# Two layers of a hybrid attention and convolution trunk: three taps of the depthwise convolution take later places on VectorE

## The chip, the cores and the metric

The kernel runs on one core of one Trainium2 chip. The metric is device time in microseconds (us) for one execution. TensorE does the matrix products, VectorE (DVE) and ScalarE (ACT) the elementwise work, GpSimd (POOL) small pieces, and SyncE (SP) issues the weight transfers.

## The reference, cut to what matters

Two layers, 512 rows of 1024 channels, float32. The change is about the order of the work of the depthwise convolution, a sum of 31 taps over each of 512 channels, and about the up-projection of latent attention, beside which some taps are computed.

```python
for l in range(DEPTH):                       # DEPTH = 2
    h = rmsnorm(x, norm_mix_g[l])
    proj = h @ w_in[l]                       # c_q, c_kv, k_r, q_b, k_b, v_b, f_logit, conv_in, gate_logit
    q_a = rmsnorm(c_q, q_norm_g[l]) @ w_uq[l]        # 384 -> 8 heads * (64 + 32 rotary)
    kv  = rmsnorm(c_kv, kv_norm_g[l]) @ w_ukv[l]     # 256 -> 8 heads * (64 keys + 64 values)
    o_a = block_attention(qa, ka, va, mla_scale, chunk_mask) @ w_bo_a[l]
    o_b = block_attention(qf, kf, vf, fox_scale, frame_mask, cum) @ w_bo_b[l]
    u = conv_in[..., :512] * sigmoid(conv_in[..., 512:])
    u = causal_depthwise_conv(u, dw_kernel[l], dw_bias[l])      # 31 taps a channel
    u = silu(layernorm(u, conv_ln_g[l], conv_ln_b[l]))
    o_c = u @ w_bo_c[l]
    y = g_a * o_a + g_b * o_b + g_c * o_c            # sigmoid gates from proj
    x = x + y @ w_out[l]
    h = rmsnorm(x, norm_ffn_g[l])
    x = x + (silu(h @ w_ffn_gate[l]) * (h @ w_ffn_up[l])) @ w_ffn_down[l]
return rmsnorm(x, final_norm_g)
```

## The kernel before

**Tiling.** Activations lie transposed: 128 channels on the partitions, 512 rows along the free dimension. A weight matrix is streamed in chunks of up to 128x1024 numbers. Each float32 number is split into a high part in a rounded matmul format and a low part, the rest, and each product is three matmuls: high by high, high by low, low by high.

**The path of a chunk.** SP loads it into one of four `raw` buffers. ScalarE casts it into one of two `w_hi` buffers (L686), once TensorE has finished the chunk that lies two before it. VectorE subtracts (L1069) and writes `w_lo`. TensorE waits for that (`lo_done`) and multiplies (L1557; in the value chunks L1609; in attention L1669). Results land in PSUM banks, and VectorE or ScalarE empties them.

**The order.** Every engine has its own list, written out by hand: there is no scheduler. A layer runs latent projections (8 chunks), convolution inputs (8), the up stage (8), attention with 18 chunks of projections mixed in, a first merge pass (28 chunks after the first 6), a second merge pass, the output projection and the feed-forward network.

**The up stage.** Its chunks are `UP` + 0 to 7. Chunks 0 and 1 give the rotary part of the queries, 2 and 3 its other part, 4 and 5 the keys (VectorE copies one tile of each, L1392, ScalarE the other, L915), 6 and 7 the values: together four tiles. In its turn c VectorE empties what it has to, then splits chunk c + 2, then computes `UP_TAPS[c]` taps. So turn 4 splits `UP` + 6, turn 5 splits `UP` + 7, turn 6 splits the first chunk of attention, and turn 7 splits nothing. Beside this GpSimd adds the rotary halves (L640), eight instructions in a row.

**The taps.** One tap is one VectorE instruction, `c_acc = u_pad[k:] * weight_k + c_acc` over 128x512 (L1146; the first tap of a channel group is L1143). There are 4 channel groups of 31 taps. Two taps in a row of one group wait for each other; of different groups they don't. All taps of the convolution stage and the up stage belong to group 0. Then `TAP_LIST` goes around the groups. The rest of the taps fill attention (`STEP_TAPS`, one to three between the softmax instructions) and 14 chunks of the first merge pass (`PASS1_TAPS`). After the last one VectorE adds the four groups (L1421) for the layer norm.

**The start of attention.** TensorE computes the scores of a step (L1624), VectorE the negated maximum (L1187), ScalarE the exponential (L780), VectorE the reciprocal and the scaling (L1157, L1159), TensorE the transposition (L1681). Three banks hold scores, so the scores of step 5 wait for the exponential of step 2. In between TensorE multiplies the projection chunks. VectorE's list has here: the maxima of steps 0 and 1, the split of the second chunk, a tap, the scaling of step 0, a tap, the scaling of step 1, a tap, and the maxima of steps 2 and 3.

The lines that pick the taps of the up stage and of the merge pass:

```python
                    if 2 <= c <= 6:
                        split(UP + c + 2)
                    for _ in range(UP_TAPS[c]):
                        tap(*next(taps_left))
...
                    split(MERGE + 2 * GATES_AHEAD + m + 2)
                    if turn is None:
                        for _ in range(PASS1_TAPS[m]):
                            tap(*next(taps_left))
```

Of the kernel before, what the change touches and what calls it, by code (L numbers as in the profile page):

```python
# [86 lines left out]


CONV_TAPS = (0, 0, 1, 1, 2, 2, 1, 0)
UP_TAPS = (0, 0, 1, 1, 0, 3, 1, 1)  # L90
LN_TURNS = 3
PASS2_TURNS = D // P // 2
CENTRE = ((), (0, 1), (2, 3), ())
# [8 lines left out]
GATES_AHEAD = 3  # L102
V_TURN_STEPS = {12: 0, 20: 1, 28: 2, 36: 3}
PASS1 = [(3, c) for c in range(4)] + [(j, c) for j in range(GATES_AHEAD) for c in (2, 3)] + [(j, c) for j in range(4, 8) for c in range(4)]
PASS1_TAPS = [3, 3, 2, 2] + [1] * 5 + [2, 5, 3, 1, 0]
STEP_TAPS = [1 + (g % 3 == 1) for g in range(62)] + [1, 1]
TAP_LIST = [(0, k) for k in range(sum(CONV_TAPS) + sum(UP_TAPS))]
TAP_LIST += [(c, k) for k in range(TAPS) for c in (1, 2, 3, 0) if (c, k) not in TAP_LIST]
STEP_TAPS[61] += CT * TAPS - sum(CONV_TAPS) - sum(UP_TAPS) - sum(PASS1_TAPS) - sum(STEP_TAPS)
assert min(STEP_TAPS) >= 0 and sum(FEED_UNITS) == 8 * len(FEED) + 6 and FEED_END[-1] == 61  # L110
# [107 lines left out]
def trunk(nc, dram, out):  # L218
# [121 lines left out]
    with ExitStack() as ctx:  # L340
# [703 lines left out]
        def _(dve):  # L1044
# [17 lines left out]
            def split(i):  # L1062

                size, kind = CHUNK_LIST[i % CHUNKS][:2]
                dve.wait_ge(hi_done, hi.add())
                h, last = w_hi[i % SPLIT], None
                for (to, of), (part, _) in zip(split_views(kind, size, w_lo[i % SPLIT], raw[i % RAW]),
                                               split_views(kind, size, h, raw[i % RAW])):
                    last = nc.vector.tensor_tensor(to, of, part.bitcast(F32), ALU.subtract)  # L1069
                last.then_inc(lo_done, 1)  # L1070
# [65 lines left out]
            def tap(c, k):  # L1136


                if taps.n % (CT * TAPS):
                    dve.wait_ge(tap_done, taps.value - (last_tile[0] not in (None, c)))  # L1140
                last_tile[0] = c
                if k == 0:
                    ins = nc.vector.tensor_scalar(c_acc[:, c, :], u_pad[:, c, 0:T], dwk_l[:, c, 0:1],  # L1143
                                                  par[:, R_DWB + c:R_DWB + c + 1], ALU.mult, ALU.add)
                else:
                    ins = nc.vector.scalar_tensor_tensor(c_acc[:, c, :], u_pad[:, c, k:k + T], dwk_l[:, c, k:k + 1],  # L1146
                                                         c_acc[:, c, :], ALU.mult, ALU.add)
                ins.then_inc(tap_done, 1)
                taps.add()
# [138 lines left out]
            for l in layers([(hi, CHUNKS - 2), (mm, EVENTS), (out_n, EVACS), (own, OWN), (taps, CT * TAPS), (sg, 4 + 24 + 22),  # L1288
# [80 lines left out]
                for c in range(UP_CH):  # L1369
# [24 lines left out]
# [4 lines that stand above are left out]
# [3 lines left out]
                for m, (j, c) in enumerate(PASS1):  # L1401
# [12 lines left out]
# [3 lines that stand above are left out]
                    if m == len(PASS1_TAPS) - 1:  # L1417
                        dve.wait_ge(tap_done, taps.value)
# [550 lines left out]
```

## Time and profile before

| | |
|---|---|
| time, median of 3 | 1721.35 us (1721.31 to 1721.38) |
| span of the profiled execution | 1719.7 us |
| TensorE busy | 1707.8 us, 99% |
| VectorE busy | 1080.4 us, 63% |
| ScalarE busy | 684.5 us, 40% |
| GpSimd busy | 195.9 us, 11% |
| share of TensorE in the chain that ended last | 94% |
| up stage to the start of attention | about 92 to 121 us in layer 0, 939 to 968 us in layer 1 |

The profile is of one execution, whose span is 1.65 us below the median of the timed runs. In a timeline, a row gives start, length, engine, line, operation and, in brackets, how long the engine stood idle before it and who ended that. Records of neighbours on one engine overlap by up to about 0.1 us, and TensorE's by more, since matmuls are pipelined: there the distance of two starts counts.

### The profile page before, as it was taken

What the parts mean: (1) busy time and instruction counts of PE and PEld (TensorE: products, weight loads), DVE (VectorE), ACT (ScalarE), POOL (GpSimd) and SP (SyncE); (2) the same over time, 40 slices, a digit from 0 to 9 for tenths busy, and PEclk for the clock granted to TensorE, in tenths of its full rate; (3) what the DMA queues carried; (4) which work ended last, traced back from release to release, by engine and by line L of the source; (5) the groups of instructions that cost most, each with busy time, mean ns of one, the idle gap of its engine ahead of it and who ended that gap; (6) DMA issues with size and microseconds to landing.
All of it is one profiled execution on the core that took longest, in us unless ns stands there. A gap on an engine that the chain in (4) does not pass through costs nothing.

```text
span 1719.7 us, 22100 instructions
## 1 busy us (share of the span) xinstructions
PE 1707.8 (99%) x7908; PEld 1367.4 (80%) x7908; DVE 1080.4 (63%) x1625; ACT 684.5 (40%) x1126; POOL 195.9 (11%) x124
## 2 busy tenths in 40 slices
PE   9999999999999999999999999999999999999998
PEld 7777777878888888888878777778788888888887
DVE  6898887966555555542359998877755555555223
ACT  4655544343343332322245554453434423333222
POOL 0831000010020000001126210000001100000010
PEclk9999999999999999999999999999999999999999
DMA  6341221433433333333243322113333333333331
GB/s 166 82 106 52 60 62 31 111 86 98 113 89 98 98 98 98 95 92 101 81 102 71 92 62 60 45 55 100 92 104 109 98 94 93 95 96 95 93 98 71
DMA packets 309909, 152.18 MB, mean 88 GB/s; under 512 B 30356, under 2 KB 309134, under 8 KB 309836
## 3 DMA queue, kind: packets, MB, share of 16 engines
q1 hardware_dynamic: 309528, 150.96, 31.7%
q8 instruction: 45, 0.74, 0.2%
q10 hardware_dynamic: 308, 0.25, 0.1%
q14 instruction: 28, 0.23, 0.0%
HBM read 149.09 MB, written 2.10 MB: 88 GB/s over the span
## 4 chain that ended last, share of the span: by engine, by line
PE 94%; DVE 3%; ACT 1%; POOL 1%; DMA 1%; issue 0%; SPq 0%; ACTq 0%; POOLq 0%; DVEq 0%
PE bank L1557 71%; PE bank L1669 12%; PE bank L1702 2%; PE bank L1681 2%; PE bank L1624 2%; PE bank L1640 1%; PE bank L1904 1%; DVE w_lo L1069 1%; PE bank L1609 1%; POOL ln_acc L566 1%; DMA raw<-in_w_in 1%; PE bank L1596 1%; PE bank L1587 0%; PE bank L1645 0%; ACT w_hi L686 0%
## 5 line engine op out<-in xcount | busy, mean ns | idle before, releaser
L686 ACT CAST w_hi<-raw 128x1024 fp32r<-128x1024 f32 (+3 forms) x311 | 295.1, 949 | 711.4 <-PE bank L1557 704.5
L1069 DVE TENSOR_TENSOR w_lo<-raw,w_hi 128x1024 fp32r<-128x1024 f32 (+3 forms) x311 | 347.2, 1116 | 205.1 <-ACT w_hi L686 203.9
L1557 PE MATMUL bank<-h_hi,w_hi 128*128 128x512 f32 x1184 | 466.3, 394 | 0.7 <-DVE w_lo L1069 0.4
L1557 PE MATMUL bank<-h_hi,w_lo 128*128 128x512 f32 x1184 | 461.1, 389 | 0.0
L1557 PE MATMUL bank<-h_lo,w_hi 128*128 128x512 f32 x1184 | 460.9, 389 | 0.0
L1557 PEld LDWEIGHTS bank<-h_hi,w_hi 128*128 128x128 f32 x1184 | 222.2, 188 | 55.4 <-issue 6.2
L1107 DVE TENSOR_TENSOR tmp<-bank,rstd_x 128x512 f32<-128x512 f32 x140 | 96.7, 690 | 260.4 <-PE bank L1557 252.8
L1557 PEld LDWEIGHTS bank<-h_lo,w_hi 128*128 128x128 f32 x1184 | 222.4, 188 | 46.9 <-issue 1.9
L1557 PEld LDWEIGHTS bank<-h_hi,w_lo 128*128 128x128 f32 x1184 | 222.3, 188 | 46.3
L1146 DVE SCALAR_TENSOR_TENSOR c_acc<-u_pad,dwk_l,c_acc 128x512 f32<-128x512 f32 x240 | 188.3, 802 | 0.4
L566 POOL TENSOR_TENSOR x_acc<-x_acc,x_sq 128x512 f32<-128x512 f32 x31 | 53.3, 1721 | 866.0 <-ACT x_sq L703 534.0
L1669 PE MATMUL bank<-h_hi,w_hi 128*128 128x512 f32 x304 | 130.9, 431 | 0.0
L1557 PE MATMUL bank<-f_hi,w_hi 128*128 128x512 f32 x330 | 128.9, 391 | 0.0
L1557 PE MATMUL bank<-f_hi,w_lo 128*128 128x512 f32 x330 | 128.5, 389 | 0.0
L1557 PE MATMUL bank<-f_lo,w_hi 128*128 128x512 f32 x330 | 128.4, 389 | 0.0
L1669 PE MATMUL bank<-h_hi,w_lo 128*128 128x512 f32 x304 | 119.0, 391 | 0.0
L1669 PE MATMUL bank<-h_lo,w_hi 128*128 128x512 f32 x304 | 118.6, 390 | 0.0
L780 ACT ACTIVATE p_b<-bank,neg_max 128x384 f32<-128x384 f32 (+3 forms) x128 | 66.8, 525 | 73.9 <-DVE neg_max L1187 72.2
L753 ACT COPY p_t<-bank 128x384 f32<-128x384 f32 (+3 forms) x128 | 49.4, 428 | 97.3 <-PE bank L1681 58.0
L1187 DVE TENSOR_REDUCE neg_max<-bank 128x1 f32<-128x384 f32 (+3 forms) x128 | 58.1, 485 | 37.7 <-PE bank L1645 24.2
L1557 PEld LDWEIGHTS bank<-f_hi,w_lo 128*128 128x128 f32 x330 | 62.0, 188 | 13.0
L1557 PEld LDWEIGHTS bank<-f_hi,w_hi 128*128 128x128 f32 x330 | 62.0, 188 | 12.7
(263 smaller groups left out, 2218.4 us busy)
## 6 DMA issues: line engine op xcount, KB each, us to landing
raw<-in_w_in SPq DMA_DIRECT2D x96, 512.0 KB, 3.8
raw<-in_w_ffn_gate SPq DMA_DIRECT2D x44, 512.0 KB, 3.7
raw<-in_w_ffn_up SPq DMA_DIRECT2D x44, 512.0 KB, 3.7
raw<-in_w_ffn_down SPq DMA_DIRECT2D x32, 512.0 KB, 3.8
raw<-in_w_out SPq DMA_DIRECT2D x16, 512.0 KB, 3.8
raw<-in_w_ffn_down SPq DMA_DIRECT2D x16, 384.0 KB, 3.4
raw<-in_w_bo_a SPq DMA_DIRECT2D x16, 256.0 KB, 2.7
raw<-in_w_bo_b SPq DMA_DIRECT2D x16, 256.0 KB, 2.7
```

Of the source, the lines that this page charges most:

```text
L566: nc.gpsimd.tensor_tensor(acc[:], acc[:], ring[i % 2][:], ALU.add).then_inc(sq_added, 1)
L686: last = nc.scalar.copy(to, of)
L753: nc.scalar.copy(to, t_bank[g % 2][:, 0:(q + 1) * P].rearrange("p (k q) -> p k q", q=P)).then_inc(turn_out, 1)
L780: nc.scalar.activation(p_b[:, p_at:p_at + w], s_bank[score_slot(step)][:, 0:w], ACT.Exp, bias=neg_max[:, step % 4:step % 4 + 1], accum_out ...
L1069: last = nc.vector.tensor_tensor(to, of, part.bitcast(F32), ALU.subtract)
L1107: return nc.vector.tensor_tensor(to, s_bank[b][rows, :], by[rows, :], ALU.mult)
L1146: ins = nc.vector.scalar_tensor_tensor(c_acc[:, c, :], u_pad[:, c, k:k + T], dwk_l[:, c, k:k + 1], c_acc[:, c, :], ALU.mult, ALU.add)
L1187: nc.vector.tensor_reduce(neg_max[:, n:n + 1], s_bank[score_slot(step)][:, 0:(q + 1) * P], AX_X, ALU.max, negate=True).then_inc(max_ready, 1)
L1557: ins = nc.tensor.matmul(bank_t[0:rows, :], wt[slot][:, w], x, start=first and k == 0 and p == 0, stop=last and k == k_tiles - 1 and p == 2)
L1624: nc.tensor.matmul(s_bank[score_slot(g)][:, 0:w], q_t[0:rows, head, q * P:w], k_t[0:rows, head, 0:w], start=True, stop=True).then_inc(scor ...
L1669: ins = nc.tensor.matmul(bank_t[:], wt[(QKV + n) % SPLIT][:, w], x, start=k == 0 and p == 0, stop=k == DT - 1 and p == 2, skip_group_check ...
L1681: ins = nc.tensor.transpose(t_bank[g % 2][:, k * P:(k + 1) * P], p_b[:, at_k:at_k + P], ident[:])
```

## The change

Two tables of numbers change. The number of taps of turns 3, 4, 5, 6 and 7 of the up stage goes from 1, 0, 3, 1, 1 to 0, 0, 1, 2, 2, so the stage has 6 taps where it had 7. The seventh goes to the merge pass, where the chunk at index 10 (the gate of branch A for block 4) gets 6 taps for 5. The number of taps in attention stays. Since group 0 now brings 13 taps from the two first stages for 14, its tap 13 stands in the around-the-groups part of the list, and taps behind it come one place later.

```diff
-UP_TAPS = (0, 0, 1, 1, 0, 3, 1, 1)
+UP_TAPS = (0, 0, 1, 0, 0, 1, 2, 2)
...
-PASS1_TAPS = [3, 3, 2, 2] + [1] * 5 + [2, 5, 3, 1, 0]
+PASS1_TAPS = [3, 3, 2, 2] + [1] * 5 + [2, 6, 3, 1, 0]
```

VectorE's list before, from the split of chunk `UP` + 5 to the second split of attention; `w_lo_59<-raw_53` is the split of `UP` + 5, `raw_54` that of 6, `raw_55` that of 7, and the 128x1024 one the split of attention's first chunk:

```order
L1069 TENSOR_TENSOR w_lo_59<-raw_53,w_hi_57 128x512
L1146 SCALAR_TENSOR_TENSOR c_acc<-u_pad,dwk_l,c_acc 128x512
L1392 COPY k_t<-bank 64x512 x2
L1069 TENSOR_TENSOR w_lo_58<-raw_54,w_hi_56 128x512
L1392 COPY k_t<-bank 64x512 x2
L1069 TENSOR_TENSOR w_lo_59<-raw_55,w_hi_57 128x512
L1146 SCALAR_TENSOR_TENSOR c_acc<-u_pad,dwk_l,c_acc 128x512 x3
L1069 TENSOR_TENSOR w_lo_58<-raw_52,w_hi_56 128x1024
L1146 SCALAR_TENSOR_TENSOR c_acc<-u_pad,dwk_l,c_acc 128x512 x2
L1187 TENSOR_REDUCE neg_max<-bank 128x1 x2
```

The same stretch of VectorE's list now:

```order
L1069 TENSOR_TENSOR w_lo_59<-raw_53,w_hi_57 128x512
L1392 COPY k_t<-bank 64x512 x2
L1069 TENSOR_TENSOR w_lo_58<-raw_54,w_hi_56 128x512
L1392 COPY k_t<-bank 64x512 x2
L1069 TENSOR_TENSOR w_lo_59<-raw_55,w_hi_57 128x512
L1146 SCALAR_TENSOR_TENSOR c_acc<-u_pad,dwk_l,c_acc 128x512
L1069 TENSOR_TENSOR w_lo_58<-raw_52,w_hi_56 128x1024
L1146 SCALAR_TENSOR_TENSOR c_acc<-u_pad,dwk_l,c_acc 128x512 x4
L1187 TENSOR_REDUCE neg_max<-bank 128x1 x2
```

No tap stands ahead of the key copies any more, one for three stands ahead of the split of attention's first chunk, and four for two between that split and the first maximum. In the first merge pass the piece of VectorE's list around the chunk at index 10 changes so:

```order
 L1107 TENSOR_TENSOR tmp_65<-bank,rstd_x 128x512
 L1069 TENSOR_TENSOR w_lo_58<-raw_54,w_hi_56 128x512
-L1146 SCALAR_TENSOR_TENSOR c_acc<-u_pad,dwk_l,c_acc 128x512 x5
+L1146 SCALAR_TENSOR_TENSOR c_acc<-u_pad,dwk_l,c_acc 128x512 x6
 L1107 TENSOR_TENSOR tmp_66<-bank,rstd_x 128x512
 L1069 TENSOR_TENSOR w_lo_59<-raw_55,w_hi_57 128x512
```

Six taps stand there in a row for five; both layers have the same pieces. The lists of TensorE, ScalarE, GpSimd and SP are the same as before.

## Rows read from the trace of the kernel before

**Rows 1.** The page: busy time of TensorE, and the chain that ended last by engine

```profile
PE 1707.8 (99%) x7908; PEld 1367.4 (80%) x7908; DVE 1080.4 (63%) x1625; ACT 684.5 (40%) x1126; POOL 195.9 (11%) x124
PE 94%; DVE 3%; ACT 1%; POOL 1%; DMA 1%; issue 0%; SPq 0%; ACTq 0%; POOLq 0%; DVEq 0%
```

**Rows 2.** Waits of TensorE, whole span: total us, times, longest us

```profile
PE bank L1624 <- ACT p_b L780: 0.9, 2, 0.5
PE bank L1609 <- DVE w_lo L1069: 0.8, 2, 0.4
```

**Rows 3.** Timeline of VectorE, layer 0, up stage to attention: start, length

```profile
103.98 1.41 DVE L1069 TENSOR_TENSOR w_lo<-raw,w_hi 128x512 fp32r<-128x512 f32 x1 [1.64 <-ACT w_hi L686]
105.32 1.78 DVE L1146 SCALAR_TENSOR_TENSOR c_acc<-u_pad,dwk_l,c_acc 128x512 f32<-128x512 f32 x1
107.02 1.38 DVE L1392 COPY k_t<-bank 64x512 f32<-64x512 f32 x2
108.32 0.68 DVE L1069 TENSOR_TENSOR w_lo<-raw,w_hi 128x512 fp32r<-128x512 f32 x1
...
110.94 2.32 DVE L1146 SCALAR_TENSOR_TENSOR c_acc<-u_pad,dwk_l,c_acc 128x512 f32<-128x512 f32 x3
113.31 1.23 DVE L1069 TENSOR_TENSOR w_lo<-raw,w_hi 128x1024 fp32r<-128x1024 f32 x1
114.45 1.53 DVE L1146 SCALAR_TENSOR_TENSOR c_acc<-u_pad,dwk_l,c_acc 128x512 f32<-128x512 f32 x2
116.02 0.62 DVE L1187 TENSOR_REDUCE neg_max<-bank 128x1 f32<-128x128 f32 x2
```

**Rows 4.** Timeline of TensorE, layer 0: first two value matmuls, scores of steps 0 and 5

```profile
109.05 0.50 PE L1609 MATMUL bank<-w_hi,c_hi 128*128 128x512 f32 x1 [0.38 <-DVE w_lo L1069]
...
109.39 0.39 PE L1609 MATMUL bank<-w_hi,c_lo 128*128 128x512 f32 x1
...
115.07 0.46 PE L1624 MATMUL bank<-k_t,q_t 100*128 100x128 f32 x2 [0.22 <-issue]
...
121.22 0.48 PE L1624 MATMUL bank<-k_t,q_t 100*128 100x256 f32 x1 [0.46 <-ACT p_b L780]
```

**Rows 5.** Timeline of ScalarE, layer 0: casts, a key copy, exponential of step 2

```profile
106.05 0.62 ACT L686 CAST w_hi<-raw 128x512 fp32r<-128x512 f32 x1 [0.90 <-PE bank L1557]
...
109.41 1.18 ACT L915 COPY k_t<-bank 64x512 f32<-64x512 f32 x2
112.22 1.06 ACT L686 CAST w_hi<-raw 128x1024 fp32r<-128x1024 f32 x1 [1.64 <-PE bank L1609]
...
120.50 0.58 ACT L780 ACTIVATE p_b<-bank,neg_max 128x384 f32<-128x384 f32 x1 [3.24 <-DVE neg_max L1187]
```

**Rows 6.** Timeline of GpSimd, layer 0: three of the eight rotary sums

```profile
103.55 1.29 POOL L640 TENSOR_TENSOR q_t<-rope_t 32x512 f32<-32x512 f32 x1
...
106.62 1.62 POOL L640 TENSOR_TENSOR q_t<-rope_t 32x512 f32<-32x512 f32 x1
...
108.31 1.83 POOL L640 TENSOR_TENSOR q_t<-rope_t 32x512 f32<-32x512 f32 x1
```

**Rows 7.** Chain of waits, layer 0: the 24 matmuls of the two value chunks

```profile
109.05 5.80 PE bank L1609 x24
```

**Rows 8.** Busy us (instructions) by engine in 116 to 121 us, then clock and DMA

```profile
116.00:121.00 5.00, 4.76 (x21) 3.30 (x19) 4.91 (x13) 1.76 (x7) 0.00 (x0) 1.00 0.70 200
```

**Rows 9.** Timelines of VectorE and TensorE, layer 1: last taps, scores of step 5

```profile
961.41 1.53 DVE L1146 SCALAR_TENSOR_TENSOR c_acc<-u_pad,dwk_l,c_acc 128x512 f32<-128x512 f32 x2
...
968.17 0.48 PE L1624 MATMUL bank<-k_t,q_t 100*128 100x256 f32 x1 [0.45 <-ACT p_b L780]
```

**Rows 10.** Timeline of VectorE in the first merge pass, layer 0, then layer 1

```profile
328.94 3.40 DVE L1146 SCALAR_TENSOR_TENSOR c_acc<-u_pad,dwk_l,c_acc 128x512 f32<-128x512 f32 x5
333.06 0.69 DVE L1107 TENSOR_TENSOR tmp<-bank,rstd_x 128x512 f32<-128x512 f32 x1 [0.73 <-PE bank L1557]
...
1180.00 0.69 DVE L1107 TENSOR_TENSOR tmp<-bank,rstd_x 128x512 f32<-128x512 f32 x1 [0.73 <-PE bank L1557]
```

## The prediction, written before the changed kernel was run

> **What bounds the kernel now.** I read the page first: TensorE is busy 99% of the span and makes up 94% of the chain that ended last [rows 1]. So a change on VectorE can only act where TensorE waits for it. I then read TensorE's waits, a list of few entries. Two belong to the stretch that the change touches, with two occurrences each, one a layer: the value chunk waits for a weight split (0.8 us together), and the scores of an attention step wait for an exponential (0.9 us) [rows 2]. The third view was the timeline of each engine around these two waits. The reader is to see two chains there.
>
> The first ends at 109.05, where TensorE starts chunk UP + 6 after 0.38 us of idle, released by VectorE's split [rows 4]. That split ran at 108.32, though ScalarE had cast its high part at 106.05 + 0.62 = 106.67 [rows 3, 5]. In front of it on VectorE stood the tap of turn 3 (105.32, and 1.78 long) and two key copies (107.02, 1.38 together).
>
> The second starts at 116.02 with the maximum of step 0. Its scores were ready at 115.07 + 0.46 = 115.53 [rows 4]; VectorE came at 116.02 because its two last taps ended at 114.45 + 1.53 = 115.98 [rows 3]. From there VectorE is busy 4.91 of 5.00 us [rows 8]: maxima, split, taps and scalings stand in an unbroken row up to the maximum of step 2. The exponential of step 2 follows (120.50), and TensorE, idle for 0.46 us, takes up the scores of step 5 at 121.22 [rows 4, 5]. So VectorE's work between the split of attention's first chunk and the first maximum is on the path already. Layer 1 has the same waits: the longest is half of the two together in both cases [rows 2], and its two last taps and its scores of step 5 have the lengths of layer 0 [rows 9].
>
> **The tap of turn 3 goes.** The key copies then follow the split of UP + 5 directly, from 103.98 + 1.41 = 105.39, and end at 105.39 + 1.38 = 106.77. The high part is there at 106.67. GpSimd, however, starts an addition at 106.62 [rows 6], a moment before VectorE can start the split. The rows show what then happens: GpSimd's addition of 103.55 took 1.29, and the split that fell on it took 1.41 where the one at 108.32 took 0.68; it ended 105.39 - 104.84 = 0.55 after GpSimd's instruction did [rows 3, 6]. The same applied to the new place gives 106.62 + 1.29 + 0.55 = 108.46 as the end of the split, for 108.32 + 0.68 = 109.00 before. TensorE starts UP + 6 some 0.05 later, at 108.5 for 109.05.
>
> The Trainium skill says so as a rule ("SBUF — State Buffer", section "Who interferes with whom"): a VectorE instruction with two SBUF inputs and a GpSimd instruction that reads SBUF exclude one another, and the one that starts second waits for the whole of the other. The trace agrees (1.41 us beside 0.68 us). Without that rule the split would end at 106.77 + 0.68 = 107.45, long before TensorE wants it. As TensorE could use only 0.1 us more, the sum would change by about that much a layer.
>
> How much TensorE gains: 0.55 us by the starts (109.05 to 108.5), 0.38 by the idle time shown. On top comes the fourth value tile, whose bank ScalarE frees at 109.41 + 1.18 = 110.59 [rows 5], and which now starts at about 108.50 + 0.34 + 8 x 0.23 = 110.68 (0.34 is the distance of the first two starts [rows 4]; the usual one is (5.80 - 0.34) / 23 = 0.237 [rows 7], some 0.23 without small waits): on time by a hair, with at most 0.1 lost. I take 0.48 us, nearer to the starts, and keep 0.38 and 0.65 (the whole distance from the undisturbed rhythm: 0.55 and the 0.11 by which 0.34 is above 0.23) as ends.
>
> **Two more taps stand between the split of attention's first chunk and the first maximum.** Before, three taps (110.94, 2.32 long) ended at 113.26, and the split started at 113.31, when ScalarE's cast (112.22 + 1.06 = 113.28) was done [rows 3, 5]. These three were covered by a wait for the cast. The cast waits for the end of UP + 6 on TensorE, so it moves by the 0.48: to 111.74, and the split to 112.83. With one tap in that place VectorE will stand idle there for over 1 us.
>
> After the split come four taps for two. All are of channel group 0 and wait for one another: three take 2.32 and two 1.53, so one more costs 0.79 [rows 3]. Two more cost 1.58. The first maximum moves by 1.58 - 0.48 = 1.10 us, from 116.02 to 117.12. Behind it queue the split, the scalings and the next maxima on VectorE, ScalarE's exponentials and TensorE's transpositions. VectorE has no slack up to the maximum of step 2 [rows 8], so the whole 1.10 reaches TensorE: the scores of step 5 at 122.32 for 121.22. TensorE arrives there 0.48 earlier and so waits 0.46 + 0.48 + 1.10 = about 2.0 us, spread over the transpositions of steps 0 and 1 and these scores. Behind that point TensorE, VectorE and ScalarE are all 1.10 later, in the same positions to each other, and nothing makes up for it, as TensorE sets the pace from there.
>
> Bounds of one layer: if TensorE gains 0.65 at UP + 6, 1.58 - 0.65 = 0.93; if it gains nothing, 1.58. I take 1.10.
>
> **The sixth tap in the merge pass.** Five taps there take 3.40, so one is 0.68; VectorE then stood idle for 0.73 until TensorE's next chunk, in both layers [rows 10]. The tap fits, with 0.05 us to spare. Cost: 0. If it did not fit, or took 1.78 as the tap of 105.32 did, it would cost up to 1.78 - 0.73 = 1.05 a layer. Transfers don't move in their order; the ones behind the splits of UP + 6 start a little earlier. The taps that change places in attention are the same number of the same kind: 0.
>
> **Sum.** Two layers x 1.10 = 2.2 us on an execution with a span of 1719.7. The median of the runs is 1721.35; the difference of 1.65 lies around the span or between executions, and I leave it as it is. 1721.35 + 2.2 = 1723.5 us. From the bounds: 1721.35 + 1.9 = 1723.2 and 1721.35 + 3.2 = 1724.5. What a measurement of this kernel can tell from no change is about 0.2%, 3.4 us; the forecast lies within it, on the slow side.
>
> **The rivals.**
>
> *The wait removed is worth more than the one grown.* If the first maximum didn't bind, because TensorE's scores of step 5 were late for another reason, the gain of 0.48 at UP + 6 would stand alone: 1721.35 - 2 x 0.48 = 1720.4. For it: TensorE is shown waiting only 0.46 there, and the chain passes through ScalarE. Against: VectorE's 4.91 of 5.00 us, and the 0.04 us between the end of the taps and the first maximum. Chance 0.10.
>
> *The split of UP + 6 falls behind two of GpSimd's additions* (slower by more than can be mistaken). If VectorE didn't get in between the additions at 106.62 and the next one, the split would end at 106.62 + 1.29 + 0.08 + 1.29 + 0.55 = 109.83, 0.83 later than before. Everything up to the first maximum moves with it: 1.58 + 0.83 = 2.41 a layer, 1721.35 + 4.8 = 1726.2. It decides if VectorE is not ready to start by 107.9, where the first addition ends. Against: it should be ready at 106.77, and in each case of the rows VectorE took its turn directly after one addition. Chance 0.05.
>
> *The sixth tap does not fit*, at its upper price of 1.05 a layer on top of the forecast: 1721.35 + 2.2 + 2.1 = 1725.6. For it: 0.05 us is thin. Against: a shortfall costs only its own size at first, and the next chunk brings VectorE another idle stretch. No GpSimd work runs there. Chance 0.05.
>
> **How the numbers follow.** The forecast has 0.80: 1723.5, with 1723.2 to 1724.5 from the bounds. I widen this downward to 1721.9, for a part of the growth hidden by slack I did not see, and up to 1724.8 for a small overrun in the merge pass. Outside stand the first rival (0.10), the second and third (0.10 together), and hardly any of the forecast's own case. Of the chances: faster by over 0.2% would need 3.4 us, which no case gives, 0.01. Slower by over 0.2% is the second and third rival cut by half for their full price, and a little of the forecast's tail: 0.06. Within 0.2%: 0.93.
>
> **What the profile of the changed kernel would show.** Right: the wait of the value chunk for a split shrinks from 0.38 to about 0.1 or less; the split of UP + 6 is about 1.8 long and ends near 108.5; four taps of 3.1 us together follow the split of 128x1024; the first maximum is near 117.1 and TensorE's scores of step 5 near 122.3, with TensorE's wait for VectorE and ScalarE at the start of attention near 2 us a layer; the row after six taps in the merge pass has an idle time close to 0, and its start moves with the rest. Wrong: a first maximum that is later with TensorE's scores of step 5 not later; a split of UP + 6 that ends after 109; or a new wait of TensorE in the merge pass.

## The result, and the profile after

| | before | changed |
|---|---|---|
| median of 17 runs | 1721.38 us (1721.21 to 1721.70) | 1725.14 us (1723.34 to 1727.00) |
| ratio | | 1.0023 (95% interval 1.0017 to 1.0030) |
| span of the profiled execution | 1719.7 us | 1723.0 us |

The change costs 3.8 us, where 2.2 were forecast, and the time lies above the range (1721.9 to 1724.8). The spread is as telling as the median. Before, all runs lie within 0.5 us. Now they form three groups: four runs from 1723.34 to 1723.48, six from 1724.82 to 1725.33, seven from 1726.64 to 1727.00. The lowest group is the forecast, 1723.5. The others are one and two times about 1.7 us above it.

Of the 88 executions of the kernel before that were timed here and beside the experiments, 87 lie between 1721.04 and 1721.75 us; one took 1726.48, with a mean granted clock of 0.948 where no run of the changed kernel is below 0.997, so it is not one of the groups above.

The profiled execution (1724.82 us) belongs to the middle group and shows both in one trace: layer 0 went as forecast, layer 1 did not. VectorE in layer 0 (start, length), to set beside [rows 3]:

```profile
103.66 1.45 DVE L1069 TENSOR_TENSOR w_lo<-raw,w_hi 128x512 fp32r<-128x512 f32 x1 [1.61 <-ACT w_hi L686]
105.03 1.38 DVE L1392 COPY k_t<-bank 64x512 f32<-64x512 f32 x2
106.38 1.79 DVE L1069 TENSOR_TENSOR w_lo<-raw,w_hi 128x512 fp32r<-128x512 f32 x1
...
112.48 1.23 DVE L1069 TENSOR_TENSOR w_lo<-raw,w_hi 128x1024 fp32r<-128x1024 f32 x1 [1.64 <-ACT w_hi L686]
113.62 3.11 DVE L1146 SCALAR_TENSOR_TENSOR c_acc<-u_pad,dwk_l,c_acc 128x512 f32<-128x512 f32 x4
116.77 0.62 DVE L1187 TENSOR_REDUCE neg_max<-bank 128x1 f32<-128x128 f32 x2
```

GpSimd beside the split at 106.38:

```profile
106.33 1.28 POOL L640 TENSOR_TENSOR q_t<-rope_t 32x512 f32<-32x512 f32 x1
```

This execution runs 0.32 us ahead of the other from its beginning (the first split here is at 103.66, there at 103.98). With that taken off, the first maximum is 116.77 + 0.32 - 116.02 = 1.07 us later, where 1.10 was forecast. The split of UP + 6 took 1.79 us: it was taken up 0.05 after GpSimd's addition and ended at 108.17, 0.56 after the addition did (107.61), where the prediction had 0.55. Four taps took 3.11.

TensorE in layer 0, to set beside [rows 4]:

```profile
108.22 0.50 PE L1609 MATMUL bank<-w_hi,c_hi 128*128 128x512 f32 x1
...
119.42 0.33 PE L1681 MATMUL bank<-ident,p_b 128*128 128x128 f32 x1
120.34 0.44 PE L1681 MATMUL bank<-ident,p_b 128*128 128x128 f32 x2 [0.59 <-DVE p_b L1159]
...
121.97 0.70 PE L1624 MATMUL bank<-k_t,q_t 100*128 100x256 f32 x2 [0.96 <-ACT p_b L780]
122.31 0.58 PE L1669 MATMUL bank<-h_hi,w_hi 128*128 128x512 f32 x1
122.74 0.40 PE L1669 MATMUL bank<-h_lo,w_hi 128*128 128x512 f32 x1
```

The value chunk starts 0.51 us earlier and without a wait shown. The scores of step 5 come 121.97 + 0.32 - 121.22 = 1.07 later. TensorE is shown idle ahead of the transposition of step 1 (0.59) and ahead of these scores (0.96), together 1.55 us where the kernel before shows 0.46. Behind them a matmul of 128x512 is 0.40 long, and they start every 0.23 us.

TensorE in layer 1, the same place:

```profile
968.26 0.44 PE L1681 MATMUL bank<-ident,p_b 128*128 128x128 f32 x2 [0.59 <-DVE p_b L1159]
...
969.88 0.70 PE L1624 MATMUL bank<-k_t,q_t 100*128 100x256 f32 x2 [0.97 <-ACT p_b L780]
970.23 0.68 PE L1669 MATMUL bank<-h_hi,w_hi 128*128 128x512 f32 x1
970.71 0.63 PE L1669 MATMUL bank<-h_lo,w_hi 128*128 128x512 f32 x1
971.13 0.63 PE L1669 MATMUL bank<-h_hi,w_lo 128*128 128x512 f32 x1
...
973.69 0.54 PE L1669 MATMUL bank<-h_hi,w_lo 128*128 128x512 f32 x1
974.07 0.40 PE L1669 MATMUL bank<-h_hi,w_hi 128*128 128x512 f32 x1
```

The idle pieces are the same. But behind them the matmuls are 0.63 long and start every 0.43 us where those of layer 0 start every 0.23. The windows of the same stretch (busy us and instructions of PE, PEld, DVE, ACT and POOL, then TensorE's granted clock as a share of full speed, DMA) say why:

```profile
962.00:966.00 4.00, 3.84 (x17) 3.14 (x18) 3.86 (x7) 2.45 (x6) 0.00 (x0) 1.00 0.50 133
966.00:970.00 4.00, 2.41 (x10) 1.12 (x10) 3.93 (x11) 0.84 (x3) 0.00 (x0) 1.00 0.49 131
970.00:971.00 1.00, 1.00 (x4) 0.85 (x5) 0.96 (x4) 0.96 (x4) 0.00 (x0) 0.79 0.00 0
971.00:972.00 1.00, 1.00 (x4) 0.71 (x4) 0.96 (x3) 0.00 (x0) 0.00 (x0) 0.50 0.00 0
...
973.00:974.00 1.00, 1.00 (x4) 0.81 (x3) 0.96 (x4) 0.31 (x2) 0.00 (x0) 0.51 0.00 0
974.00:975.00 1.00, 1.00 (x7) 0.77 (x7) 0.96 (x4) 0.00 (x0) 0.00 (x0) 1.00 0.00 0
```

The granted clock is 0.50, the lower of TensorE's two levels, 1.2 for 2.4 GHz, from the middle of 970 to 971 until about 974. Ahead of it TensorE was busy 2.41 of 4.00 us. (In layer 0 it was busy 2.41 of the 4.00 us from 118.10 to 122.10 too, and there the clock stayed at 1.00.) In the chain of waits the twelve matmuls behind the scores of step 5 show the price. Layer 0 of the changed kernel, then layer 1 (start, length):

```profile
122.67 2.75 PE bank L1669 x12
...
970.58 4.35 PE bank L1669 x12
```

4.35 - 2.75 = 1.60 us is, but for 0.1, the distance of 1.7 between two groups of runs. In the kernel before, TensorE was busy 4.73 of the 5.00 us from 963 to 968, and 3.55 of the 4.00 us from 964.30 to 968.30, which hold its idle of 0.45, with the clock at 1.00 throughout:

```profile
963.00:968.00 5.00, 4.73 (x21) 3.30 (x19) 4.93 (x13) 1.76 (x7) 0.00 (x0) 1.00 0.72 203
968.00:972.00 4.00, 3.83 (x19) 3.24 (x20) 3.89 (x13) 2.19 (x11) 0.00 (x0) 1.00 0.00 1
```

In the first merge pass, VectorE beside [rows 10]:

```profile
329.68 4.06 DVE L1146 SCALAR_TENSOR_TENSOR c_acc<-u_pad,dwk_l,c_acc 128x512 f32<-128x512 f32 x6
333.81 0.69 DVE L1107 TENSOR_TENSOR tmp<-bank,rstd_x 128x512 f32<-128x512 f32 x1
```

Times here are the trace's own, 0.74 later than before at this place (329.68 for 328.94). The next product is taken up at 333.81, for 333.06 + 0.74 = 333.80: the sixth tap cost nothing. In layer 1 it is the same: six taps from 1179.19, the next product at 1183.32, with no wait for TensorE shown between them.

### The profile page after: what moved, and what is told of

Its sections match the earlier page's. It is cut to its first block, busy times and chain, and to the rows that moved or that the text cites. A ratio compares the mean times of both kernels' runs of the same rounds, so it can differ in the third digit from the quotient of the medians.

```text
span 1723.0 us, 22100 instructions
## 1 busy us (share of the span) xinstructions
PE 1709.0 (99%) x7908; PEld 1367.7 (79%) x7908; DVE 1080.7 (63%) x1625; ACT 685.0 (40%) x1126; POOL 194.9 (11%) x124
## 4 chain that ended last, share of the span: by engine, by line
PE 95%; DVE 2%; ACT 1%; POOL 1%; DMA 1%; issue 0%; SPq 0%; ACTq 0%; POOLq 0%; DVEq 0%
PE bank L1557 72%; PE bank L1669 12%; PE bank L1702 2%; PE bank L1681 2%; PE bank L1624 2%; PE bank L1640 1%; PE bank L1904 1%; DVE w_lo L1069 1%; POOL ln_acc L566 1%; DMA raw<-in_w_in 1%; PE bank L1596 1%; PE bank L1587 0%; PE bank L1645 0%; ACT w_hi L686 0%; PE bank L1609 0%
```

## The experiments

Theory A: the longer idle of TensorE at the start of attention, 1.55 us shown for 0.46 (the expectations below call it 2.04, as the prediction's sum had it), makes the clock fall there in a share of the executions, in each layer by itself. Theory B: the fall has another cause in the change, such as the earlier start of the value chunks, or comes at random whatever the idle. The comparisons below are each with the kernel before on the same chip; its median was 1721.33 to 1721.39 in all of them. The early tap alone, the late part alone, three taps and the idle filled in both pieces ran on one chip; five taps, the second piece alone filled, one late tap fewer and both gains together on another; the last run on a third. The changed kernel itself was not run again beside them.

**Only the tap of turn 3 moved.**

```diff
-UP_TAPS = (0, 0, 1, 1, 0, 3, 1, 1)
+UP_TAPS = (0, 0, 1, 0, 0, 3, 1, 1)
...
-PASS1_TAPS = [3, 3, 2, 2] + [1] * 5 + [2, 5, 3, 1, 0]
+PASS1_TAPS = [3, 3, 2, 2] + [1] * 5 + [2, 6, 3, 1, 0]
```

> Only the tap of turn 3 leaves the up stage (for the sixth place in the merge pass); turns 5, 6, 7 keep 3, 1, 1. Both theories: chunk UP + 6 starts about 0.5 us earlier and, with two taps behind the split of attention's first chunk as before, so does the first maximum. 2 x 0.5 off 1721.35: 1720.4 us. TensorE's idle before the scores of step 5 stays 0.46 us. Theory A (TensorE's clock falls after the longer idle at the start of attention): no drop of the clock, runs within 0.3 us of one another. Theory B (the drop comes from the earlier start of the value chunks or from anything else that the change does, not from the idle): groups of runs 1.6 us apart as in the changed kernel.

Measured: 1720.32 us (1720.04 to 1720.57, 11 runs), ratio 0.9992 (0.9983 to 1.0001). In the medians the gain is 0.5 us a layer, as the first wait promised, but the interval just includes 1. There are no groups. TensorE's waits in this kernel (total us, times, longest):

```profile
PE bank L1624 <- ACT p_b L780: 0.9, 2, 0.5
```

The second wait is as before [rows 2], and the value chunk's wait is gone from the list. So the early part of the change does not make the clock fall by itself, and by the medians and the trace it is a gain.

**Only the late part.**

```diff
-UP_TAPS = (0, 0, 1, 1, 0, 3, 1, 1)
+UP_TAPS = (0, 0, 1, 1, 0, 1, 2, 2)
```

> Only the late part: turns 5, 6, 7 have 1, 2, 2 taps, the tap of turn 3 stays, the merge pass has its five. The first maximum comes 2 x 0.79 = 1.58 us later than before in each layer, nothing is gained at UP + 6. TensorE's idle at the start of attention is 0.46 + 1.58 = 2.04 us, as in the changed kernel. With the clock kept: 1721.35 + 3.2 = 1724.5 us. Theory A: the clock falls in some layers of some runs, so runs stand in groups near 1724.5, 1726.2 and 1727.8, median about 1726. Theory B (the early tap's removal is needed): all runs near 1724.5.

Measured: 1727.54 us, seven runs: two at 1725.87 and 1725.95, five from 1727.34 to 1727.82; ratio 1.0032 (1.0021 to 1.0043). The groups are there without the early part: theory B in its first form is out. The profiled execution (span 1724.1, of the lower group) has the clock down once, in layer 1:

```profile
970.00:975.00 5.00, 4.04 (x13) 3.22 (x13) 4.89 (x14) 2.72 (x10) 0.00 (x0) 0.71 0.14 43
```

No run is at 1724.5, the time with the clock kept; by the groups each has the fall in one layer or in both, 12 of 14 chances. In the profiled execution the clock fell at about 972.1, 1.1 us after the scores of step 5 were taken up (970.98), with three matmuls of 128x512 already started at full speed. From the first matmul of 128x512 in attention to the scores of 100x384 behind the whole stretch it is 976.62 - 964.33 = 12.29 us in layer 1 and 126.57 - 115.89 = 10.68 in layer 0, so this fall cost 1.61.

**Three taps for four ahead of the first maximum.**

```diff
-UP_TAPS = (0, 0, 1, 0, 0, 1, 2, 2)
+UP_TAPS = (0, 0, 1, 0, 0, 2, 1, 2)
```

(against the changed kernel)

> Turns 5, 6, 7 have 2, 1, 2 taps: three taps between the split of attention's first chunk and the first maximum, where before has two and the changed kernel four. The first maximum moves by 0.79 - 0.5 = 0.3 us a layer, TensorE's idle there is about 0.46 + 0.79 = 1.25 us. Clock kept: 1721.35 + 0.6 = 1722.0 us. Theory A: with an idle this much shorter the clock falls rarely or never, so a narrow group at 1722.0. Theory B: groups 1.6 us apart as in the changed kernel.

Measured: 1721.90 us (1721.71 to 1722.05, 11 runs), ratio 1.0002 (0.9992 to 1.0011); one narrow group at the time forecast with the clock kept. TensorE in the same four microseconds of layer 1:

```profile
966.00:970.00 4.00, 2.97 (x13) 1.79 (x13) 3.93 (x11) 1.80 (x6) 0.00 (x0) 1.00 0.48 131
```

The idle ahead of the scores of step 5 in the same layer:

```profile
968.63 0.70 PE L1624 MATMUL bank<-k_t,q_t 100*128 100x256 f32 x2 [0.97 <-ACT p_b L780]
```

TensorE was busy 2.97 of 4.00 us, between the 2.41 of the changed kernel and the 3.55 of the kernel before, and the clock stayed. The wait ahead of the scores is the changed kernel's, 0.97 us; the one of 0.59 ahead of the transposition is gone. So the longer of the two pieces alone did not bring the clock down in 11 runs. One tap fewer in each layer takes away about its own 0.79 ((1723.4 - 1721.9) / 2 = 0.75) and, in these runs, the falls with it.

**The idle filled.** The changed kernel, and in TensorE's list:

```diff
+FILL = (2, 4)
...
                         latent_logits(g)
+                        if g == 4:
+                            busy(FILL[1])
                         latent_logits(g + 1)
...
+                def busy(times):
+                    for _ in range(times):
+                        nc.tensor.matmul(o_bank[:, 0:P], ones[:], ones[:], start=True, stop=True)
...
                     turn(g)
+                    if g == 0:
+                        busy(FILL[0])
                     turn(g + 1)
```

> The changed kernel with six small matmuls on TensorE (128x128 of ones into the bank that attention's output uses later, results unused): two ahead of the transposition of step 1 and four ahead of the scores of step 5, in the two longest idle pieces (0.59 and 0.97 us). Each takes about 0.2 us, so nothing waits longer. Theory A: with the idle filled the clock stays, all runs at 1723.4 us, the changed kernel's lowest group. Theory B: the groups at 1723.4, 1725.1 and 1726.8 stay. If the six cost their own 1.2 us a layer, 1725.8.

Measured: 1723.36 us (1723.20 to 1723.77, 11 runs), ratio 1.0010 (1.0001 to 1.0019). All are in the changed kernel's lowest group. VectorE's order, and so the lateness of the chain, is the changed kernel's (the scores of step 5 start 122.11 - 118.50 = 3.61 us after the pair of scores ahead of them, as 121.97 - 118.36 in the changed kernel); only TensorE's idle differs. TensorE in layer 0 (L1689 are the added matmuls, each of which has two records, so two show as x4 and four as x8):

```profile
119.56 0.33 PE L1684 MATMUL bank<-ident,p_b 128*128 128x128 f32 x1
119.73 0.61 PE L1689 MATMUL bank<-ones 128*128 128x128 f32 x4
120.48 0.44 PE L1684 MATMUL bank<-ident,p_b 128*128 128x128 f32 x2
120.76 0.39 PE L1625 MATMUL bank<-k_t,q_t 100*128 100x128 f32 x2
120.98 1.06 PE L1689 MATMUL bank<-ones 128*128 128x128 f32 x8
```

The run with only the late part stood beside this one on the same chip, and none of its seven runs was at the time with the clock kept. With this, theory B falls in both its forms, and TensorE's idle is shown to be the cause: work whose result nobody uses makes the kernel 1.8 us faster in the median.

**Only the second piece of idle filled.** As above with `FILL = (0, 4)`.

> The changed kernel with only the four small matmuls ahead of the scores of step 5, which fill most of its 0.97 us of idle; the 0.59 us ahead of the transposition of step 1 stays open. Theory A with the sum of the idle stretches as what counts: about 1.2 us left, the clock stays, all runs at 1723.4 us. If the first stretch alone is enough to start the drop, groups at 1723.4, 1725.1 and 1726.8 stay.

Measured: 1723.48 us (1723.28 to 1723.64, 11 runs), ratio 1.0012 (1.0003 to 1.0021). The 0.59 us ahead of the transposition may stay open: that piece alone did not bring the clock down in 11 runs, on the chip on which no run of the kernel with five taps (below) was at its time with the clock kept. The kernel with three taps has the other piece alone, and kept the clock too. The changed kernel has both, with 0.7 us between them, and loses it in a share of its runs.

**Five taps ahead of the first maximum.**

```diff
-UP_TAPS = (0, 0, 1, 0, 0, 1, 2, 2)
+UP_TAPS = (0, 0, 1, 0, 0, 0, 2, 3)
```

(against the changed kernel)

> Turns 5, 6, 7 have 0, 2, 3 taps: five taps between the split of attention's first chunk and the first maximum. The maximum comes 3 x 0.79 - 0.5 = 1.87 us later than before in each layer, TensorE's idle there is 0.46 + 2.37 = 2.83 us. Clock kept: 1721.35 + 3.7 = 1725.1. Theory A: the drop is at least as frequent as with 2.04 us of idle, so most runs have both, at 1725.1 + 3.3 = 1728.4. Theory B (the clock does not follow the idle): groups as often at 1725.1 as at 1728.4.

Measured: 1727.88 us, five runs, three from 1727.70 to 1727.88 and two at 1729.25 and 1729.64; ratio 1.0043 (1.0029 to 1.0056). Theory A's direction holds, as no run is at 1725.1, but its size of a fall does not, and neither does its group at 1728.4: the profiled execution has the fall in layer 1 alone and yet a span of 1725.9. It starts in the idle ahead of the scores of step 5 (970.64 to 971.60), at about 970.8, and lasts longer, until about 977.6:

```profile
967.00:972.00 5.00, 2.75 (x10) 1.31 (x9) 4.93 (x12) 1.77 (x7) 0.00 (x0) 0.89 0.38 105
972.00:976.00 4.00, 4.00 (x10) 3.09 (x10) 3.89 (x12) 1.59 (x8) 0.00 (x0) 0.50 0.00 0
...
977.00:978.00 1.00, 1.00 (x6) 0.72 (x5) 0.25 (x1) 0.00 (x0) 0.00 (x0) 0.65 0.00 0
```

So 1.6 us is not a fixed price. Between the same two places as in the run with only the late part, layer 1 takes 978.49 - 964.17 = 14.32 us and layer 0 takes 126.95 - 115.48 = 11.47: this fall cost 2.85. (1727.8 less the 1725.1 worked out for the clock kept gives some 2.7.) TensorE was busy only 1.75 of the 4.00 us ahead of the scores in both layers, and layer 0 kept the clock even so. What the runs at 1729.25 and 1729.64 had is not shown, as neither was profiled.

**One late tap fewer than before.**

```diff
-UP_TAPS = (0, 0, 1, 1, 0, 3, 1, 1)
+UP_TAPS = (0, 0, 1, 1, 0, 3, 1, 0)
```

(with the six at index 10 of the merge pass)

> Turns 3 and 5 keep 1 and 3 taps, turn 7 has none, so one tap for two stands behind the split of attention's first chunk; the merge pass has six. VectorE could start the first maximum 0.79 us earlier, at 115.2 by its own list, but the scores of step 0 are ready at 115.53 and those of step 1 at 115.98. If VectorE's list is what the scores of step 5 wait for, the 0.46 us of idle of TensorE there goes: 2 x 0.4 to 0.46 less, 1720.5 us. If TensorE's scores of step 0 set the start of the chain, nothing is gained: 1721.35.

Measured: 1721.17 us (1720.99 to 1721.41, 11 runs), ratio 0.9999 (0.9990 to 1.0008). Of the two times expected this is, within 0.2 us, the one without a gain, 1721.35. VectorE in layer 0:

```profile
114.46 0.75 DVE L1146 SCALAR_TENSOR_TENSOR c_acc<-u_pad,dwk_l,c_acc 128x512 f32<-128x512 f32 x1
115.65 0.79 DVE L1187 TENSOR_REDUCE neg_max<-bank 128x1 f32<-128x128 f32 x2 [0.44 <-PE bank L1624]
```

VectorE now waits for the scores, 0.44 us, and the pair of maxima ends at 116.44 for 116.64 [rows 3], as the second needs the scores of step 1. In the kernel before, the last taps ended at 115.98 [rows 3] and the four matmuls of the scores of steps 0 and 1, 0.91 us from 115.07 in its chain of waits, at 115.98 too: two bounds at one place, and taking one away shows the other. TensorE's wait ahead of the scores of step 5 only shrinks from 0.46 to 0.36.

**Both together.**

```diff
-UP_TAPS = (0, 0, 1, 1, 0, 3, 1, 1)
+UP_TAPS = (0, 0, 1, 0, 0, 3, 1, 0)
...
-PASS1_TAPS = [3, 3, 2, 2] + [1] * 5 + [2, 5, 3, 1, 0]
+PASS1_TAPS = [3, 3, 2, 2] + [1] * 5 + [3, 6, 3, 1, 0]
```

> The tap of turn 3 and one late tap leave the up stage (turns 3 to 7: 0, 0, 3, 1, 0); the merge pass gets three at index 9 and six at index 10, where VectorE stood idle for 1.27 and 0.73 us. The two gains add up if the reading of both waits is right: 2 x (0.5 + 0.45) off 1721.35, 1719.4 us, no drop of the clock. If the idle of one wait only moves to the other, 1720.4.

Measured: 1720.06 us (1719.95 to 1720.43, 11 runs), ratio 0.9993 (0.9984 to 1.0002). This is neither of the times expected, 1719.4 for two gains that add up and 1720.4 for one: it is the early tap's 1.0 us and some 0.3 for the late one, near the 0.2 of the run above. TensorE still waits 0.38 us ahead of the scores of step 5. The interval just includes 1.

**The chain made shorter behind the maxima.** The kernel with only the early tap moved, and:

```diff
+STEP_TAPS[1] -= 1
...
-PASS1_TAPS = [3, 3, 2, 2] + [1] * 5 + [2, 6, 3, 1, 0]
+PASS1_TAPS = [3, 3, 2, 2] + [1] * 5 + [3, 6, 3, 1, 0]
```

> e1_early_tap with one tap fewer in the first step pair of attention, between the scaling of step 1 and the maximum of step 2; it goes to index 9 of the first merge pass. If VectorE's unbroken row up to the maximum of step 2 is what TensorE's scores of step 5 wait for, this row is 0.46 us shorter (the distance of the starts 119.45 and 119.91), and TensorE's 0.46 us of idle go: 1720.3 - 2 x 0.4 = 1719.5 us. If something else sets that wait, the time stays at 1720.3.

Measured: 1719.39 us (1719.25 to 1719.63, 11 runs), ratio 0.9989 (0.9980 to 0.9998). The wait of the scores of step 5 for an exponential is gone from TensorE's waits, both layers. This is the best version of the study, 2.0 us below the kernel before and 5.8 below the changed one. The interval is clear of 1. It also confirms the reading of the chain: VectorE's unbroken row up to the maximum of step 2 was what TensorE waited for.

## Why the prediction was wrong

**Which waits matter, and by how much: right.** The earlier start of UP + 6 was forecast with 0.48 us a layer and measured with 0.5 (0.51 in the trace, 1.0 us for two layers in the run of the early tap alone). The split that meets GpSimd's addition was forecast to end at 108.46; it ended at 106.38 + 1.79 + 0.32 = 108.49. The wait of the value chunk is gone.

**Two more taps: right.** Forecast 1.58 us a layer, and 1.10 net for the first maximum and for TensorE's scores of step 5; measured 3.11 - 1.53 = 1.58, and 1.07 in layer 0. The "about 2.0 us" of TensorE's wait is not what the profile shows, 1.55: the distance from the pair of scores ahead to those of step 5 did grow by 0.51 + 1.07 = 1.58 (3.61 for 2.03), but part of it lies in matmuls that no longer overlap in the trace, so the 0.46 and the 1.58 do not add up in shown idle. That does not move the sum. The sum without any clock was 1723.5; four of 17 runs of the changed kernel, and all 22 with the idle filled, in one piece or both, are at 1723.2 to 1723.8.

**The sixth tap in the merge pass: right**, 0.

**"Behind that point TensorE, VectorE and ScalarE are all 1.10 later, in the same positions to each other": wrong.** This step took TensorE's speed behind the idle as given. The prediction worked out that TensorE would wait "about 2.0 us" there and priced that idle at its own length alone. The granted clock then fell to half, and a fall in the changed kernel costs 1.6 us more, a term that stood in the sum at nothing. Read from the groups (only one execution was profiled, with one fall), the runs are at 1723.4, 1725.1 and 1726.8 with a fall in neither, one or both layers; 6 x 1 + 7 x 2 = 20 of the 34 chances (17 runs, two layers) had it, 20 / 34 x 1.6 = 0.94 us a layer on average. 2 x 1.07 + 2 x 0.94 = 4.0 us, which is the difference of the means (1725.4 and 1721.4); that of the medians is 3.8. The Trainium skill has the mechanism ("TensorE: Matmul & The Clock Gate", section "What's actually happening": activity releases a throttle whose default is the lower clock), and I read none of the rivals from it. The rows agree in direction: the clock falls to the lower level behind the longer idle and stays up where the idle is filled. The rows of before could not show it, since the clock is at 1.00 in that stretch [rows 8] and at 90% or more in every slice of the page; but the idle of 2.0 us, four times the longest that this stretch had, was in my own sum.

**The rivals.** None of the three happened. The split did not fall behind a second addition, the tap in the merge pass fitted, and the first maximum did bind, as it and the scores of step 5 both came 1.07 later. One reading that was incomplete but did no harm to the sum: the prediction had the start of the maxima bound by VectorE's taps alone, and the run with one late tap fewer showed the scores of step 1 as a second bound at the same place, 115.98.

**What stays open.** Why the same program with the same idle keeps the clock in one execution or layer and loses it in another. All three profiled executions with a fall (the changed kernel, the late part only, five taps) have it in layer 1 alone; in which layer the other runs had it is not known. Layer 0 of the run with five taps kept the clock with the longest idle of all (busy 1.75 of 4.00 us), so a longer idle does not settle it either. The Trainium skill says in the same section that the monitor runs freely and is not tied to the kernel's start, by which the phase would decide; our runs agree in that only a share of the executions falls, but none of them sets the phase. How far the idle may grow between the kernel with three taps (no fall in 11 runs) and the changed kernel (20 of 34 chances) was not measured more finely. Nor is it shown whether the late part alone falls more often (12 of 14) for a reason or by chance.

## What to carry to other kernels

When a change lets TensorE stand idle longer in one place, price the idle twice: once its length, and once the chance that the matmuls behind it run at half the clock. Groups in the runs' times, a fixed distance apart, are a sign of it; the granted clock in narrow windows behind the longest waits proves it, and a mean over the whole span (0.998) hides it. Look at pieces of idle that lie close together as one: here each alone did no harm and both together did.

Where filling work is moved past a dependent instruction, count the instructions between the last thing that engine waits for and the first that others wait for. Here VectorE's three taps were free ahead of the split, and two of them cost their full 0.79 us each behind it. Before taking work away from there, look for a second bound at the same place.

## What the runs showed of the hardware

- TensorE's idle of 0.59 us alone (the second piece filled) and of 0.97 us alone (three taps) each left all 11 runs in one narrow group, at the time with the clock kept. Both, 0.7 us apart, were followed by a granted clock of 0.50 for some 3.4 us in a share of the executions.
- Four small matmuls a layer whose results are not used keep the granted clock: the groups at 1725.1 and 1726.8 are gone (11 of 11 runs at 1723.3 to 1723.6), at no cost of their own beside 1723.4.
- The size of a fall is not fixed: 1.6 us where it began with the first matmuls of 128x512 behind the idle (changed kernel) or three of them later (late part only), 2.85 us where it began inside the idle of the kernel with five taps and lasted 6.8 us.
- A VectorE subtraction with two inputs in SBUF (128x512) took 0.68 us alone and 1.79 where GpSimd's addition of 1.28 had started 0.05 before it; it ended 0.56 after the addition.
- A chain of taps that depend on one another goes at 0.79 us a tap, taps of different channel groups at 0.66 (six in 4.06 us for five in 3.40 [rows 10]).
